# RWKV-7 chain of a hybrid block: stacked 128-row operands, loads in two parts, token operands by head half

## The chip, the cores and the metric

The kernel runs on one core of a Trainium2 chip. Its time is the device time of one execution in microseconds (us); lower is better. The kernel before takes 5299.23 us (median of 3 runs).

## What is computed

A block: one layer over 2048 latent tokens and 256 context tokens: a token mixer with two groups of heads side by side (HGRN2 and RWKV-7, each in both directions), an output projection, and a mixture of experts. The change touches the RWKV-7 part alone: 8 heads of 64, each with a 64x64 state, walked forward and backward.

```python
def rwkv7_scan(r, w, k, v, kk, a, s0):
    def step(s, inp):
        rt, wt, kt, vt, kkt, at = inp
        sa = jnp.einsum('nbhij,nbhj->nbhi', s, kkt)
        s = (s * wt[..., None, :] - sa[..., :, None] * (kkt * at)[..., None, :]
             + vt[..., :, None] * kt[..., None, :])
        return s, jnp.einsum('nbhij,nbhj->nbhi', s, rt)
...
def rwkv7_readout(y, r, k, v, g, r_k, gn_w, gn_b):
...
    yn = ((y - mu) * lax.rsqrt(var + RW_GN_EPS)).reshape(y.shape[:-2] + (D_RW,)) * gn_w + gn_b
    bonus = jnp.sum(r * k * r_k, -1, keepdims=True) * v
    return (yn + bonus.reshape(bonus.shape[:-2] + (D_RW,))) * g
```

## The kernel before

Everything is float32; one matmul shows as two records in the profile. The stages follow one another: modulation, RWKV projection, HGRN projection beside RWKV preparation (`RwkvPrep`), the two scans side by side (`scans`, about 1,540 to 3,240 us of the span), readout (`Readout`), experts, combination.

**Preparation** writes two scratch tensors to DRAM. `s_rw_in` holds, per direction and chunk of 64 tokens, rows of 1028 numbers with the channel (two heads of 64, a "pair") on 128 partitions: alpha, rho, decay, beta, kappa. `s_rw_tm` holds the token-major operands (64 tokens by beta, kappa, v, 512 channels each).

**The RWKV scan** (`RwkvScan`) takes 36 steps of 64 tokens, each for two directions d = 0 and 1. Heads lie in 4 pairs j; half h = 0 or 1 of a pair is on partitions 0 to 63 or 64 to 127. The body for step n does two things: it builds the operands and the triangular inverse of step n (`gram0`, `gram1`, `turn`, then `cross` and `grow` for levels 1 to 5), and runs the state chain of step n-1 on the other set of buffers (`rhs`, `solve`, `out`, `state`):

- `rhs`: alpha times state plus masked kappas times v (L1370, L1372), copied by ScalarE (ACT);
- `solve`: inverse times rhs gives u (L1381), copied by ScalarE (L1488);
- `out`: rho times state, plus kappas times v, plus A_rho_beta times u (L1391, L1393, L1395);
- `state`: kappa tokens times v plus beta tokens times u (L1405, L1407); VectorE (DVE) adds the state (L1583) and multiplies by the decay (L1585).

`mask(d, 1)` on VectorE (L1560, to `rw_kappas`) masks what `gram1` (L1422) left in PSUM, in one instruction; `turn` (L1431) waits for it. GpSimd (POOL) makes the level masks of the inverse (L1544), VectorE its first level (L1569) and its later ones (L1575).

**The HGRN scan** is interleaved on all engines: 18 steps, one per two RWKV steps, from a quarter of the first of the two bodies on. Its scores (L429) need operands scaled by GpSimd (L411, L412), from exponents by VectorE (L474) and ScalarE (L379, L380).

**Order.** The order on each engine is a list of positions (`RW_ORDER`, below) merged with the HGRN tasks when the program is built; every engine runs its own list in order and waits on semaphores. A loop iteration holds four RWKV and two HGRN steps. Below, an *even body* is one with u = 0, an *odd body* one with u = 1; the HGRN output phase ends just ahead of an even body.

```python
RW_ORDER = ("gram0 rhs gram1 turn cross1 solve grow1 cross2 out grow2 cross3 grow3 state cross4 grow4 cross5 grow5").split()
```

**Loads.** SyncE (SP) issues the loads of step n once `s_ready` says that VectorE has finished the state of body n-1: per direction one DMA of `rw_operands` (128 rows of 4112 bytes) and two of `rw_tokens` (pieces of 256 bytes), all counted on one semaphore, for which `gram0` waits.

## Time and profile before

| | |
|---|---|
| median of 3 runs | 5299.23 us (5294.71 to 5325.04) |
| the profiled execution, its own time | 5331.71 us |
| its span in the trace | 5329.8 us |
| granted TensorE clock, mean over the span | 0.913 of full speed |
| TensorE (PE) busy | 4381.7 us, 82% |
| VectorE busy | 2250.0 us, 42% |
| ScalarE busy | 1214.9 us, 23% |
| GpSimd busy | 1510.6 us, 28% |

Busy time is the union of an engine's instructions. Records of matmuls overlap, so the time that a matmul adds is read from the distance of the starts of consecutive groups, not from the duration of one.

### The profile page before, as it was taken

The numbers are of one execution on the slowest core, as the hardware profiler recorded it, in microseconds if no ns is written. First come the engines' busy times: TensorE is split into PE (matmuls) and PEld (weight loads), VectorE is DVE, ScalarE is ACT, GpSimd is POOL, SyncE is SP. The second block draws the span as 40 slices with busy tenths as digits, with TensorE's granted clock in tenths as the row PEclk, the third lists the DMA queues.
The fourth block names the chain that finished last, engine by engine and source line by source line (L and its number), as shares of the span: only waits on it lengthen the run. The fifth ranks groups of instructions, "written<-read, shape, count | busy, mean of one in ns | idle before, by whom it ended". The sixth has DMA issues, their size and how long they took to land. (4 is left out here: it accounts for less than half of the span.)

```text
span 5329.8 us, 123036 instructions
## 1 busy us (share of the span) xinstructions
PE 4381.7 (82%) x47298; PEld 2984.8 (56%) x47298; DVE 2250.0 (42%) x4072; ACT 1214.9 (23%) x3101; POOL 1510.6 (28%) x1933
## 2 busy tenths in 40 slices
PE   3998799899969888988888885875699999999950
PEld 1877666666658777877777773443233333333320
DVE  1112176666644544544445444887111111111138
ACT  0001044443433333333333332321000000000000
POOL 0000011011125544545445453443222212222210
PEclk7999899999989999999999997987899999999975
DMA  9312255555533232232322325432757798887864
GB/s 302 126 58 71 67 184 194 163 179 187 167 94 90 70 82 62 70 90 70 88 60 68 89 70 149 141 132 82 291 228 283 323 370 365 363 364 325 340 242 185
DMA packets 365510, 917.20 MB, mean 172 GB/s; under 512 B 181121, under 2 KB 220417, under 8 KB 332065
## 3 DMA queue, kind: packets, MB, share of 16 engines
q1 hardware_dynamic: 310208, 760.24, 41.2%
q0 software_dynamic: 47392, 133.02, 7.1%
q10 hardware_dynamic: 7488, 17.83, 0.9%
q8 instruction: 326, 5.34, 0.4%
q14 instruction: 96, 0.78, 0.0%
HBM read 951.35 MB, written 211.26 MB: 218 GB/s over the span
## 5 line engine op out<-in xcount | busy, mean ns | idle before, releaser
L2405 PE MATMUL exp_gate_up<-exp_w_gate,exp_rows_and_rowsT 128*64 128x512 f32 x1664 | 773.2, 624 | 89.9 <-DMA exp_w_up<-in_moe_w_up_dram 89.0
L2405 PE MATMUL exp_gate_up<-exp_w_up,exp_rows_and_rowsT 128*64 128x512 f32 x1664 | 773.9, 624 | 0.0
L2405 PEld LDWEIGHTS exp_gate_up<-exp_w_gate,exp_rows_and_rowsT 128*64 128x64 f32 x1664 | 235.9, 144 | 592.7 <-issue 592.7
L1544 POOL TENSOR_TENSOR rw_A_level<-rw_A_rho_beta,const_level_masks 128x256 f32<-128x256 f32 x432 | 336.7, 795 | 705.4 <-DVE rw_A_rho_beta L1560 428.8
L721 PE MATMUL rwp_product<-rwp_hT,rwp_w_rw 128*128 128x256 f32 (+1 forms) x2016 | 443.9, 383 | 0.0
L874 PE MATMUL hgp_product<-hgp_hT,const_w_hg 128*128 128x256 f32 x1728 | 410.4, 394 | 26.6 <-DMA hgp_hT<-s_hT 15.8
L2359 DVE TENSOR_TENSOR exp_hidden<-exp_hidden,exp_gate_up 64x512 f32<-64x512 f32 x104 | 71.9, 692 | 821.9 <-ACT exp_hidden L2340 821.9
L721 PEld LDWEIGHTS rwp_product<-rwp_hT,rwp_w_rw 128*128 128x128 f32 (+1 forms) x2016 | 380.9, 189 | 61.2
L874 PEld LDWEIGHTS hgp_product<-hgp_hT,const_w_hg 128*128 128x128 f32 x1728 | 337.6, 199 | 87.8 <-DMA hgp_hT<-s_hT 16.3
L2429 PE MATMUL exp_down<-exp_w_down,exp_hiddenT 128*64 128x512 f32 x1664 | 380.0, 598 | 1.1
L1575 DVE TENSOR_TENSOR rw_inverse<-rw_inverse,rw_inverse_bank 128x512 f32<-128x512 f32 x288 | 196.5, 685 | 356.8 <-PE rw_inverse_bank L1454 354.8
L2340 ACT ACTIVATE exp_hidden<-exp_gate_up 64x512 f32<-64x512 f32 x104 | 61.2, 588 | 1075.1 <-PE exp_gate_up L2405 1075.1
L2313 POOL DMA_INDIRECT s_yb<-exp_out,exp_row_slot x104 | 104.2, 1002 | 677.2 <-PE exp_rows_turned L2391 552.2
L1451 PE MATMUL rw_inverse_bank<-rw_inverse,rw_X 64*64 64x64 f32 x5760 | 246.2, 227 | 60.3 <-ACT rw_X L1504 40.2
L1443 PE MATMUL rw_inverse_bank<-rw_inverse,rw_A_level 64*64 64x64 f32 x5760 | 231.9, 222 | 45.8 <-DVE rw_inverse L1575 37.3
L1451 PEld LDWEIGHTS rw_inverse_bank<-rw_inverse,rw_X 64*64 64x64 f32 x5760 | 211.1, 140 | 74.2 <-issue 68.0
L411 POOL TENSOR_TENSOR hg_scaled_qk<-hg_qkf,hg_exponent 128x256 f32<-128x256 f32 x252 | 217.3, 862 | 121.7 <-ACT hg_exponent L380 121.4
L871 PE MATMUL hgp_product<-const_w_hg,hgp_hT 128*128 128x512 f32 x576 | 251.6, 592 | 0.0
L2009 PE MATMUL read_projected<-read_w_out,read_mixT 128*128 128x512 f32 x512 | 235.9, 621 | 4.1 <-DVE read_w_out L1874 2.9
L1504 ACT ACTIVATE rw_X<-rw_inverse_bank 128x256 f32<-128x256 f32 x360 | 135.2, 380 | 452.9 <-PE rw_inverse_bank L1443 447.3
L1443 PEld LDWEIGHTS rw_inverse_bank<-rw_inverse,rw_A_level 64*64 64x64 f32 x5760 | 199.0, 135 | 67.2 <-issue 58.9
L2405 PEld LDWEIGHTS exp_gate_up<-exp_w_up,exp_rows_and_rowsT 128*64 128x64 f32 x1664 | 235.8, 144 | 0.0
(385 smaller groups left out, 7942.8 us busy)
## 6 DMA issues: line engine op xcount, KB each, us to landing
exp_w_gate<-in_moe_w_gate_dram SPq DMA_DIRECT2D x104, 2048.0 KB
exp_w_up<-in_moe_w_up_dram SPq DMA_DIRECT2D x104, 2048.0 KB
exp_w_down<-in_moe_w_down_dram SPq DMA_DIRECT2D x104, 2048.0 KB
s_rw_in<-prep_operands SPq DMA_DIRECT2D x72, 514.0 KB, 4.1
rw_operands<-s_rw_in SPq DMA_DIRECT2D x72, 514.0 KB, 5.5
rw_tokens<-s_rw_tm SPq DMA_DIRECT2D x144, 192.0 KB, 6.6
hg_qkf<-s_hg_in SPq DMA_DIRECT2D x36, 768.0 KB, 7.9
mod_w<-in_w_mod_dram SPq DMA_DIRECT2D x24, 1024.0 KB, 26.1
```

The costliest lines, as they stand in the source:

```text
L411: nc.gpsimd.tensor_tensor(zk, level_views(k, d, l)[1], dk, ALU.mult)
L721: mm = nc.tensor.matmul(mp[o % 2][0:width, 0:GROUP], w_in[:, k, c0 - 5 * D_HG:c0 - 5 * D_HG + width], hT[b][:, k, :], start=(k == 0), stop ...
L871: mm = nc.tensor.matmul(self.mp[o % 4][:], self.hT[b][:, k, j * P:(j + 1) * P], self.w[:, k, c0:c0 + D_HG], start=(k == 0), stop=(k == KD ...
L874: mm = nc.tensor.matmul(self.mp[o % 4][:, 0:GROUP], self.w[:, k, c0:c0 + P], self.hT[b][:, k, :], start=(k == 0), stop=(k == KD - 1))
L1443: i = nc.tensor.matmul(self.pa[d][q, 0, j, :], self.al[d][l % 2][q, j, :], self.rt[u][d][q, 1, j, :], start=True, stop=True)
L1451: i = nc.tensor.matmul(self.pa[d][q, 0, j, :], self.x[d][q, j, :], self.rt[u][d][q, 0, j, :], start=True, stop=True)
L1504: nc.scalar.activation(self.x[d][:], self.pa[d][:, 0], ACT.Copy).then_inc(s["x_ready"], 1)
L1544: nc.gpsimd.tensor_tensor(self.al[d][l % 2][:], self.ar[u][d][:, :, 0, :], self.K["lvc"][:, d, l, :].unsqueeze(1).broadcast_to([P, NPAIR, ...
L1575: V.tensor_tensor(rt[:], rt[:], self.pa[d][:], ALU.add).then_inc(s["r_ready"], 1)
L2009: mm = self.nc.tensor.matmul(self.py[j][:], self.mT[:, k, :], self.w_out[:, k, j * 512:(j + 1) * 512], start=(k == 0), stop=(k == KD - 1))
L2405: i = nc.tensor.matmul(pgu[u][q:q + BLK], xT[:, k, r * BLK:(r + 1) * BLK], w[r][:, k, :], start=(k == 0), stop=(k == KD - 1))
L2429: i = nc.tensor.matmul(pd[u][c * 64 + x:c * 64 + x + BLK], hT[u][:, k, x:x + BLK], wd[r][:, k, c * 512:(c + 1) * 512], start=(k == 0), sto ...
```

## The change

Instead of two or three matmuls with 64 rows that add up in PSUM, one matmul with 128 rows takes both terms, with the operands stacked on the partitions. Per step and direction:

- `lead` holds, for half h of each pair, alpha and rho on that half's partitions and the masked kappas on the other half's; `sv` holds state over v, `uv` u over v, `tk` beta tokens over kappa tokens. `rhs` falls from 16 matmuls to 8, `out` from 24 to 16 (8 with 128 rows, then 8 with 64 for the u term, pair by pair), `state` from 16 to 8. `gram1` writes to the other half's partitions.
- The mask of the kappas becomes two VectorE instructions of 64 partitions, the state's add and decay two each, ScalarE's copy of u two.
- A step's loads are 22 DMAs in place of 6. Alpha and rho are issued after `y_ready`, the rest of the row after `s_ready`, then for both directions the tokens with a semaphore of their own, for which only the next body's `rhs` waits. v is loaded twice.
- `s_rw_tm` is laid out by operand and head half (pieces of 1 KB). ScalarE's copies in the preparation write in that order; the readout loads v in it and adds the bias into a new tile `v_bias`.

```diff
-        self.row = two(lambda u, d: sb(f"operands{u}{d}", [P, ROW]))
-        self.tm = two(lambda u, d: sb(f"tokens{u}{d}", [P, 3, NPAIR, RW_C]))
+        self.lead = two(lambda u, d: sb(f"alpha_rho_over_kappas{u}{d}", [P, 2, 2, NPAIR, RW_C]))
+        self.row = two(lambda u, d: sb(f"decay_beta_kappa{u}{d}", [P, ROW - 2 * XW]))
+        self.tk = two(lambda u, d: sb(f"beta_over_kappa_tokens{u}{d}", [P, 2, NPAIR, RW_C]))
+        self.sv = two(lambda u, d: sb(f"state_over_v{u}{d}", [P, 2, NPAIR, RW_C]))
+        self.uv = two(lambda u, d: sb(f"u_over_v{u}{d}", [P, 2, NPAIR, RW_C]))
...
     def sync(self, sp, n, u):
...
+            wait(sp, s["y_ready"], n - 1)
+            row = S["rw_in"][d, bass.ds(n, 1)].rearrange("n p x -> p (n x)")
+            for h in range(2):
+                sp.dma_start(self.lead[u][d][HALF[h], h].rearrange("p x j t -> p (x j t)"), row[HALF[h], 0:2 * XW]).then_inc(got, 16)
             wait(sp, s["s_ready"], n - 1)
...
+            sp.dma_start(self.row[u][d][:], row[:, 2 * XW:]).then_inc(got, 16)
+        for d in range(2):
+            tok = S["rw_tm"][d, bass.ds(n, 1)].rearrange("n x h s e -> x h s (n e)")
             for h in range(2):
...
+                for x in range(2):
+                    sp.dma_start(self.tk[u][d][HALF[h ^ x], h].rearrange("s j e -> s (j e)"), tok[x, h]).then_inc(self.tokens[u][d], 16)
+                for v in (self.sv, self.uv):
+                    sp.dma_start(v[u][d][HALF[1 - h], h].rearrange("s j e -> s (j e)"), tok[2, h]).then_inc(self.tokens[u][d], 16)
...
         def rhs(d):
...
+            pe.wait_ge(self.tokens[w][d], self.got_tokens(n - 1, w))
             pe.sem_inc(self.turns, 1)
...
+            for j, h, q in places:
+                i = nc.tensor.matmul(self.pb[d][q, 0, j, :], self.lead[w][d][:, h, 0, j, :], self.sv[w][d][:, h, j, :], start=True, stop=True)
...
         def out(d):
...
+                for _, h, q in places[0:2]:
+                    nc.tensor.matmul(o[q, 0, j, :], self.lead[w][d][:, h, 1, j, :], self.sv[w][d][:, h, j, :], start=True, stop=False)
+                for _, h, q in places[0:2]:
+                    i = nc.tensor.matmul(o[q, 0, j, :], self.ar[w][d][q, j, 1, :], self.uv[w][d][q, h, j, :], start=False, stop=True)
...
         def mask(d, k):
...
+            for h in range(2):
+                q = HALF[1 - h]
+                i = V.tensor_tensor(self.lead[u][d][q, h].rearrange("p x j t -> p j x t"), grams[q],
+                                    K["bu"][q, d].unsqueeze(1).broadcast_to([RW_C, NPAIR, 2, RW_C]), ALU.mult)
+            i.then_inc(s["masked"], 1)
...
         def state(d):
...
+            for h in range(2):
+                q = HALF[h]
+                V.tensor_tensor(self.st[d][q], self.sv[w][d][q, h], self.pb[d][q, 1], ALU.add).then_inc(s["s_order"], 1)
+            dve.wait_ge(s["s_order"], 2 * n)
+            for h in range(2):
+                q = HALF[h]
+                i = V.tensor_tensor(self.sv[u][d][q, h], self.st[d][q], self.row[w][d][q, 0:NPAIR].unsqueeze(2).broadcast_to([RW_C, NPAIR, RW_C]),
+                                    ALU.mult)
```

TensorE at the start of `out(0)` in an even body. Before: the last two cross products (direction 0 and 1), then one pair's three terms of two matmuls each, which repeat for the other pairs and direction 1.

```order
L1443 MATMUL rw_inverse_bank0<-rw_inverse00,rw_A_level00 64x64 x8
L1443 MATMUL rw_inverse_bank1<-rw_inverse01,rw_A_level10 64x64 x8
L1391 MATMUL rw_chain_bank0<-rw_state0,rw_operands10 64x64 x2
L1393 MATMUL rw_chain_bank0<-rw_tokens10,rw_kappas10 64x64 x2
L1395 MATMUL rw_chain_bank0<-rw_u0,rw_A_rho_beta10 64x64 x2
```

After: the same two cross products, then one 128-row term and one 64-row term per pair, in turn.

```order
L1455 REGISTER_ALU
L1458 MATMUL rw_inverse_bank0<-rw_inverse00,rw_A_level00 64x64 x8
L1458 MATMUL rw_inverse_bank1<-rw_inverse01,rw_A_level10 64x64 x8
L1413 MATMUL rw_chain_bank0<-rw_state_over_v10,rw_alpha_rho_over_kappas10 64x64 x2
L1415 MATMUL rw_chain_bank0<-rw_u_over_v10,rw_A_rho_beta10 64x64 x2
```

The three terms of a pair became two, and kinds with 128 and 64 rows alternate eight times per direction.

SyncE between the state of one body and the next HGRN loads (L353). Before, one step's loads for both directions:

```order
L1343 DMA rw_operands<-s_rw_in 128x1028
L1345 DMA rw_tokens<-s_rw_tm 64x12x64 x2
L1343 DMA rw_operands<-s_rw_in 128x1028
L1345 DMA rw_tokens<-s_rw_tm 64x12x64 x2
L353 DMA hg_qkf<-s_hg_in 128x3x512
```

After, the same stretch:

```order
L1356 DMA rw_alpha_rho_over_kappas<-s_rw_in 64x512 x2
L1358 DMA rw_decay_beta_kappa<-s_rw_in 128x516
L1356 DMA rw_alpha_rho_over_kappas<-s_rw_in 64x512 x2
L1358 DMA rw_decay_beta_kappa<-s_rw_in 128x516
L1363 DMA rw_beta_over_kappa_tokens<-s_rw_tm 64x256 x2
L1365 DMA rw_state_over_v<-s_rw_tm 64x256
L1365 DMA rw_u_over_v<-s_rw_tm 64x256
```

The three kinds of token rows at the end stand four times in a row, once per direction and half; then come the HGRN loads, L353. So the tokens stand behind both directions' rows now.

VectorE at the start of an even body, from the mask of `gram0` to the first later level of the inverse. Before:

```order
L1560 TENSOR_TENSOR rw_A_rho_beta<-rw_inverse_bank,const_before_upto 128x512 x2
L1569 TENSOR_TENSOR rw_inverse<-rw_A_level,const_ident 128x256 x2
L1560 TENSOR_TENSOR rw_kappas<-rw_inverse_bank,const_before_upto 128x512 x2
L1575 TENSOR_TENSOR rw_inverse<-rw_inverse,rw_inverse_bank 128x512 x2
L497 SCALAR_TENSOR_TENSOR hg_logf_sum<-const_chunk_starts,hg_logf 128x512 x2
```

After:

```order
L1578 TENSOR_TENSOR rw_A_rho_beta<-rw_inverse_bank,const_before_upto 128x512 x2
L1593 TENSOR_TENSOR rw_inverse<-rw_A_level,const_ident 128x256 x2
L1583 TENSOR_TENSOR rw_alpha_rho_over_kappas<-rw_inverse_bank,const_before_upto 64x4x2x64 x4
L1599 TENSOR_TENSOR rw_inverse<-rw_inverse,rw_inverse_bank 128x512 x2
L497 SCALAR_TENSOR_TENSOR hg_logf_sum<-const_chunk_starts,hg_logf 128x512 x2
```

The mask of the kappas has four instructions for its two, ahead of the same work.

## Rows read from the trace of the kernel before

**Rows 1.** The page, part 1: busy time and share of the span.

```profile
PE 4381.7 (82%) x47298; PEld 2984.8 (56%) x47298; DVE 2250.0 (42%) x4072; ACT 1214.9 (23%) x3101; POOL 1510.6 (28%) x1933
```

**Rows 2.** Windows, the scan without its ends: busy time by engine, clock, DMA share.

```profile
1560.00:3220.00 1660.00, 1457.52 (x34204) 1295.12 (x34203) 814.04 (x1438) 573.27 (x1500) 863.94 (x1070) 0.95 0.28 73
```

**Rows 3.** Waits in the same stretch: us in total, times, longest.

```profile
PE rw_inverse_bank L1451 <- ACT rw_X L1504: 40.2, 18, 2.4
...
PE rw_inverse_bank L1422 <- DMA rw_tokens<-s_rw_tm: 35.2, 19, 2.8
...
PE rw_inverse_bank L1431 <- DVE rw_kappas L1560: 10.6, 15, 1.4
```

**Rows 4.** Timeline, TensorE, 16-record groups: start, length, line, tile shape, count.

```profile
2352.07 0.63 PE L1451 MATMUL rw_inverse_bank<-rw_inverse,rw_X 64*64 64x64 f32 x16
2352.53 0.63 PE L1454 MATMUL rw_inverse_bank<-rw_X,rw_inverse 64*64 64x64 f32 x16
2353.10 0.69 PE L429 MATMUL hg_score_psum<-hg_scaled_qk 128*64 128x64 f32 x16
2353.71 0.68 PE L1451 MATMUL rw_inverse_bank<-rw_inverse,rw_X 64*64 64x64 f32 x16
2354.23 0.63 PE L1454 MATMUL rw_inverse_bank<-rw_X,rw_inverse 64*64 64x64 f32 x16
```

**Rows 5.** Timeline, TensorE in the HGRN output phase, where the tile shape changes.

```profile
2371.28 0.43 PE L452 MATMUL hg_out_psum<-hg_v,hg_scores_across 128*64 128x128 f32 x2
2371.64 0.43 PE L454 MATMUL hg_out_psum<-hg_v,hg_scores 64*64 64x128 f32 x4
```

**Rows 6.** Timeline, TensorE, two terms of `out`.

```profile
2394.52 0.31 PE L1391 MATMUL rw_chain_bank<-rw_state,rw_operands 64*64 64x64 f32 x4
2394.64 0.31 PE L1393 MATMUL rw_chain_bank<-rw_tokens,rw_kappas 64*64 64x64 f32 x4
```

**Rows 7.** Timeline, the start of an even body, by engine.

```profile
2385.33 1.80 DVE L1569 TENSOR_TENSOR rw_inverse<-rw_A_level,const_ident 128x256 f32<-128x256 f32 x2 [0.33 <-POOL rw_A_level L1544]
...
2385.67 1.92 PE L1422 MATMUL rw_inverse_bank<-rw_operands 64*64 64x128 f32 x32
...
2387.05 1.28 DVE L1560 TENSOR_TENSOR rw_kappas<-rw_inverse_bank,const_before_upto 128x512 f32<-128x512 f32 x2
...
2387.88 1.24 PE L1431 MATMUL rw_inverse_bank<-const_ident,rw_inverse 64*64 64x64 f32 x32 [0.29 <-DVE rw_kappas L1560]
```

**Rows 8.** Timeline, the start of an odd body, by engine.

```profile
2421.49 1.09 PE L1422 MATMUL rw_inverse_bank<-rw_operands 64*64 64x128 f32 x16 [2.15 <-DMA rw_tokens<-s_rw_tm]
2421.87 0.84 POOL L412 TENSOR_TENSOR hg_scaled_qk<-hg_qkf,hg_exponent 128x256 f32<-128x256 f32 x1
...
2423.44 0.69 PE L429 MATMUL hg_score_psum<-hg_scaled_qk 128*64 128x64 f32 x16
...
2427.02 0.69 DVE L1560 TENSOR_TENSOR rw_kappas<-rw_inverse_bank,const_before_upto 128x512 f32<-128x512 f32 x1 [1.37 <-PE rw_inverse_bank L1422]
...
2427.89 0.69 DVE L1560 TENSOR_TENSOR rw_kappas<-rw_inverse_bank,const_before_upto 128x512 f32<-128x512 f32 x1 [0.18 <-PE rw_inverse_bank L1422]
...
2428.40 1.15 PE L1431 MATMUL rw_inverse_bank<-const_ident,rw_inverse 64*64 64x64 f32 x32
```

**Rows 9.** Timeline, VectorE around the state of an even body.

```profile
2410.07 0.43 DVE L1585 TENSOR_TENSOR rw_state<-rw_state,rw_operands 128x256 f32<-128x256 f32 x1
...
2412.32 0.69 DVE L1575 TENSOR_TENSOR rw_inverse<-rw_inverse,rw_inverse_bank 128x512 f32<-128x512 f32 x1 [0.90 <-PE rw_inverse_bank L1454]
```

**Rows 10.** DMA issues in the scan: KB each, median us from issue to landing.

```profile
rw_operands<-s_rw_in SPq DMA_DIRECT2D x68, 514.0 KB, 5.1
rw_tokens<-s_rw_tm SPq DMA_DIRECT2D x136, 192.0 KB, 6.5
```

**Rows 11.** Windows, ten microseconds around an odd body's load wait.

```profile
2326.00:2336.00 10.00, 7.56 (x126) 6.69 (x123) 5.13 (x10) 1.78 (x6) 5.06 (x8) 0.83 0.41 94
```

**Rows 12.** Timeline, the first matmuls of the scan.

```profile
1543.38 1.97 PE L1422 MATMUL rw_inverse_bank<-rw_operands 64*64 64x128 f32 x16 [35.35 <-DMA rw_tokens<-s_rw_tm]
```

91 lines of the change are left out of this document (41 added, 50 removed).

## Prediction

> **What bounds the kernel now.** I read the page first: TensorE is busy 82% of the span, no other engine over 42% [rows 1]. The change lies in the scan, so the next view is the window of 1560 to 3220 us: TensorE 1457.5 of 1660 us busy, VectorE 814, GpSimd 864, ScalarE 573, DMA share 0.28, clock 0.95 [rows 2]. TensorE leads, but it isn't alone. It runs one list in order, and its gaps name three others: ScalarE's `rw_X` 40.2 us, a load 35.2 us, the mask of the kappas 10.6 us [rows 3]. So each edit has two prices, in TensorE's stream and in the wait that ends last near it, and I read one even body and one odd body as timelines for the second.
>
> **TensorE's stream.** In `out` the next term starts 0.117 us after four records, that is two 64-row matmuls: 0.058 us for a matmul [rows 6]. A group of 16 records (8 matmuls) takes 0.46 to 0.47 us start to start in one tile shape [rows 4]. The 128-row price is in the HGRN scores: L429 has 128x64 tiles, 64 columns wide, in alternate halves, just as the new matmuls. Around it the distances are 0.46, 0.57, 0.61 and 0.52 us [rows 4]. Against 0.467 that is 0.30 too much for two changes of tile shape, so a stacked matmul costs the same 0.058 us, and a change of shape 0.15 us. The HGRN output confirms this: four 64-row records of 128 columns, or two of 128 rows, take 0.36 us there [rows 5], where `gram` pays about 0.056 us a record (32 records in about 1.8 us) and so 0.225 for four; the rest, 0.14, is the change of shape.
>
> I counted both programs' lists over one loop iteration (four steps): 1936 matmuls become 1744, and changes of shape rise from 113 to 179. 192 x 0.058 = 11.2 us are saved, 66 x 0.15 = 9.9 us are added. Net -1.3 us per four steps, -12 us over the scan's nine iterations. By place, per body: `out` saves 8 x 2 x 0.058 = 0.93 us and adds 16 changes (15 in an odd body, where L429 stands ahead), +1.3 to +1.5 us. `rhs` and `state` each save 0.93 us less 0.30 us for the changes, or the whole 0.93 where L429 stands beside them.
>
> The page "TensorEngine Tiling (Array Packing)" of the Trainium skill, section "Restrictions and Gotchas", says that row tiles can't access the same PSUM bank at once. By it the pairs of 64-row tiles would take turns and the stacked ones not, so that the 192 stacked matmuls per iteration would take half: 192 x 0.029 x 9, a further 50 us off. Rows 4 speak against it: L1451 (64 rows) and L429 (128 rows) go at one pace. Its section "Tiling Modes" says that a change of tile within a mode needs no drain, which is what the `gram1` that writes across does; no run here shows such a tile. The nearest rows bound that edit between 0 and 0.15 us a change, and I take 0, since the shape is the same.
>
> **The mask split in two.** `turn` waits for it. In the even body VectorE is in L1569 until 2387.13, starts the masks at 2387.05 and ends them 1.28 us later; `turn` starts at 2387.88, 0.14 us behind the first one's end [rows 7]. Two masks are 1.28 us with 0.69 each [rows 8], so one more costs 0.60. The half-height ones have the same length per partition; I take the full 0.60 us each (0.30 would be in proportion to partitions, no row shows it). Two more make the second `turn` 1.2 us later. The time that a shorter `rhs` gives is lost here too: `gram1` ends earlier, but VectorE, not TensorE, is late (L1569 waited for GpSimd [rows 7]). Even body up to `turn`: +1.2 us.
>
> **The load wait.** In odd bodies the second `gram0` waits for the tokens, 2.15 us in the row, 1.85 us on the mean of 19 [rows 3, 8]. After the change it waits only for the row, issued ahead of the tokens; a row lands 5.1 us after issue, tokens 6.5 [rows 10]. The state of the even body ends at 2410.5 [rows 9], so the rows land by about 2417.5, ahead of 2419.3, where the wait began. The wait goes. Next late is the HGRN: L429 at 2423.44 needs L412, which ends at 2422.71 [rows 8], and that doesn't move. So only 0.6 of the 2.15 us come through, and the shorter first `rhs` brings nothing more. Then the second `rhs` saves 0.35 us, `gram1` begins near 2424.9, the masks run from 2425.95 to 2428.45, and the second `turn` starts at 2428.55, where it started at about 2428.95 (half of the 1.15 us behind 2428.40). Odd body up to `turn`: -0.4 us. Where the clock fell around the wait (0.83 granted over ten microseconds [rows 11], the lower level for a third of them) more comes back, for all was twice as long; I saw this in about 8 of 18, at 1.5 us, -12 us in all.
>
> **State.** TensorE's 0.93 us saved stands ahead of HGRN scores that wait themselves, so I keep half. VectorE has eight instructions for four; the second of a pair adds about 0.35 us, 1.3 us a body. Behind them are HGRN exponents and the inverse of level 4, which had 0.90 us of slack [rows 9]: +0.3 us. The page "SBUF — State Buffer" of the Trainium skill says that a VectorE operation with two SBUF inputs and a GpSimd one lock each other out; the multiplication has two such inputs. The row agrees in kind (L1569 took 0.90 us a piece beside GpSimd, [rows 7]). By it the split would cost up to 1 us more a body.
>
> **Edits taken at nothing.** ScalarE's second copy of u (0.4 us a piece) lies 3 us ahead of `out`, under `grow1` and `cross2`. 22 DMAs for 6 on SyncE: their tokens are needed a body later, and the HGRN loads behind them half a body later; if a DMA costs 0.5 us to issue that is 11 us of 47 a body. In preparation and readout the same elements move in another order, beside a busy TensorE. At the scan's start the first `gram0` comes with the row in place of the tokens, 1.4 us sooner [rows 10, 12], and the second doesn't wait (some 1.85 us): -3 us.
>
> **The sum.** Even body: +1.2 (turn) +1.5 (out) -0.5 (state, half) +0.3 (VectorE) = +2.5 us. Odd body: -0.4 +1.3 -0.5 +0.3 = +0.7 us. 18 of each: +58 us; less 12 (clock) and 3 (start): +43 us. Some of what I add will fall into waits that were there (`rw_X` 40.2 us, [rows 3]), though its ScalarE work starts behind `out` and so moves along; I take off a quarter, 11 us. Forecast **+32 us**: the profiled execution's 5331.7 would be 5364, the median 5299 would be 5331.
>
> **Rivals.**
> - *TensorE's stream decides and the waits vanish.* -12 us of stream, -35 of load wait, -12 of clock, -3 at the start, masks hidden: -62, 5237 us. For it: TensorE is the busiest. Against it: in both timelines another engine ends last at `turn` and L429. Chance 0.12.
> - *Split instructions land on the chain in full* (slower). Each body pays the masks (1.2 us even; 0.7 odd, where they start 0.87 us apart and `turn` had some 0.2 us), VectorE's state (1.3) and `out` (1.5, 1.3), and keeps nothing of `rhs` and `state`: 18 x (4.0 + 3.3) = +131; less 15 (clock, start) and 11 (0.6 us of the load wait in 18 bodies) and the same quarter: +79, 5378 us. It decides from the point where VectorE's extra 2.5 us a body exceeds its slack. Chance 0.22.
> - *The changes of shape cost little in short groups*, say half: -66 x 0.075 x 9 = -45 from the forecast, 5286 us. The price is from groups of 2 to 16 records, so it is well held. Chance 0.14.
> - *PSUM rule* (the page above): 5281 us. Chance 0.02.
> - The forecast, near 5331: chance 0.50.
>
> **How the numbers follow.** Under 1% (53 us) this kernel's runs can't tell from no change. The forecast's own spread (a state saving kept or lost, VectorE at 0.3 to 1.3 us) is +-30 us. The range runs from 5255, which leaves out most of the first rival, to 5395, which takes in most of the second. Faster by over 1% (under 5246): 0.13. Slower by over 1% (over 5352): a quarter of the forecast's own chance and most of the second rival's, 0.34. Within: 0.53.
>
> **What would show it.** Right: the load wait of `gram0` gone; waits on the kappa mask up from 10.6 us to 40 or more; groups in `out` 0.26 us apart; new waits ahead of L429 in odd bodies. Wrong: masks of half height near 0.3 us; groups in `out` 0.12 to 0.2 us apart; the scan shorter by tens of microseconds with the waits on VectorE unchanged; or a clock that falls more often, since `out` now leaves gaps in the array.

## The result and the profile after

The changed kernel takes 5378.72 us (median of 4 runs, 5366.24 to 5383.47), the kernel before 5297.33 us (4 runs). By the medians that is 81 us more; the ratio is 1.0143, 95% interval 1.0119 to 1.0168, that is 76 us (63 to 89), where 32 was forecast. The sign was right, the forecast less than half of what came; the time fell on the slower rival (5378).

The page, part 1, of the kernel after, and windows over the whole scan, before and after:

```profile
PE 4364.3 (81%) x43842; PEld 2940.6 (55%) x43842; DVE 2392.4 (44%) x4290; ACT 1247.9 (23%) x3173; POOL 1528.3 (28%) x1933
...
1543.38:3232.28 1688.90, 1481.12 (x34551) 1314.68 (x34553) 820.97 (x1454) 577.15 (x1509) 869.87 (x1078) 0.95 0.29 75
1540.12:3291.22 1751.10, 1468.49 (x31152) 1267.85 (x31152) 961.98 (x1666) 609.50 (x1580) 886.40 (x1078) 0.94 0.26 78
```

From the first `gram0` to the end of the last `solve` the scan takes 1751.1 us where it took 1688.9: +62. In it TensorE is busy only 13 us less, for all the matmuls saved, and VectorE 141 us more; the granted clock is 0.94 for 0.95. This scan length is the measure for the experiments below. It comes from one profiled execution of each kernel, and that of the kernel before (5331.71) lies 34 us over its median, where the others lie at most 11 us from theirs; so set beside its 1688.9 another kernel looks somewhat faster than it is. The start comes 3.3 us sooner, as forecast (3), and what stands behind the scan is 9.5 us shorter in these two profiles, which the change doesn't touch beyond the readout.

The waits of TensorE from 1560 to 3220 us, as in [rows 3], of the kernel after (us in total, times, longest; the last 71 us of the scan lie behind this stretch):

```profile
PE rw_inverse_bank L1458 <- DVE rw_inverse L1599: 85.7, 94, 2.8
PE rw_inverse_bank L1466 <- ACT rw_X L1521: 42.5, 18, 2.4
PE rw_inverse_bank L1446 <- DVE rw_alpha_rho_over_kappas L1583: 41.5, 31, 1.8
PE rw_inverse_bank L1437 <- issue: 30.3, 7, 5.3
PE rw_inverse_bank L1446 <- issue: 27.8, 37, 1.4
```

The load wait of [rows 3], 35.2 us, is gone, and the wait for `rw_X` is what it was (40.2). Three others have come or grown: `turn` (L1446) waits for the kappas' mask (10.6 before) and, in the row "issue", for its second half; the `cross` products (L1458) wait for the inverse (L1599); and `gram0` (L1437) stands still seven times for nothing that these rows name, once per loop iteration (10.7 us in seven times before).

The start of an even body, the place of [rows 7], in the timeline after:

```profile
2416.18 1.80 DVE L1593 TENSOR_TENSOR rw_inverse<-rw_A_level,const_ident 128x256 f32<-128x256 f32 x2 [0.34 <-POOL rw_A_level L1561]
2418.01 2.81 DVE L1583 TENSOR_TENSOR rw_alpha_rho_over_kappas<-rw_inverse_bank,const_before_upto 64x512 f32<-64x512 f32 x4
2419.55 0.68 PE L1446 MATMUL rw_inverse_bank<-const_ident,rw_inverse 64*64 64x64 f32 x16 [1.75 <-DVE rw_alpha_rho_over_kappas L1583]
2420.93 0.68 PE L1446 MATMUL rw_inverse_bank<-const_ident,rw_inverse 64*64 64x64 f32 x16 [0.70 <-issue]
```

Four half masks take 2.81 us where two whole ones took 1.28: (2.81 - 0.69) / 3 = 0.71 us apart, not 0.60. The second `turn` starts 2.92 us behind the first mask. Before, its 32 records had no gap.

`out` (0.26 us a term, as forecast), from the timeline after, and below it the state section of an odd body:

```profile
2427.14 0.34 PE L1413 MATMUL rw_chain_bank<-rw_state_over_v,rw_alpha_rho_over_kappas 128*64 128x64 f32 x4
2427.41 0.33 PE L1415 MATMUL rw_chain_bank<-rw_u_over_v,rw_A_rho_beta 64*64 64x64 f32 x4
...
2441.12 1.10 PE L1423 MATMUL rw_chain_bank<-rw_u_over_v,w_beta_over_kappa_tokens 128*64 128x64 f32 x32
2442.16 0.68 PE L1458 MATMUL rw_inverse_bank<-rw_inverse,rw_A_level 64*64 64x64 f32 x16
...
2442.43 0.86 DVE L1609 TENSOR_TENSOR rw_state_sum<-rw_state_over_v,rw_chain_bank 64x256 f32<-64x256 f32 x2
2443.32 0.85 DVE L1613 TENSOR_TENSOR rw_state_over_v<-rw_state_sum,rw_decay_beta_kappa 64x256 f32<-64x256 f32 x2
2444.20 0.87 DVE L1609 TENSOR_TENSOR rw_state_sum<-rw_state_over_v,rw_chain_bank 64x256 f32<-64x256 f32 x2
2445.10 1.28 DVE L1613 TENSOR_TENSOR rw_state_over_v<-rw_state_sum,rw_decay_beta_kappa 64x256 f32<-64x256 f32 x2
2446.42 0.69 DVE L474 TENSOR_TENSOR hg_exponent<-hg_logf_sum 128x512 f32<-128x512 f32 x1
...
2447.48 1.27 DVE L1599 TENSOR_TENSOR rw_inverse<-rw_inverse,rw_inverse_bank 128x512 f32<-128x512 f32 x2
2448.40 1.19 PE L1458 MATMUL rw_inverse_bank<-rw_inverse,rw_A_level 64*64 64x64 f32 x32 [1.85 <-DVE rw_inverse L1599]
```

TensorE's state product is now 1.04 us from start to start, a saving; but VectorE needs from 2442.43 to 2446.38 for the eight halves, each as long as the whole instruction of [rows 9]. Then come an HGRN exponent and the inverse. In [rows 9], of an even body, VectorE waited 0.90 us at this point for TensorE; now TensorE waits 1.85 us for VectorE.

The start of an odd body, the place of [rows 8]:

```profile
2451.96 1.96 PE L1437 MATMUL rw_inverse_bank<-rw_alpha_rho_over_kappas,rw_decay_beta_kappa 64*64 64x128 f32 x32
2454.93 0.69 PE L429 MATMUL hg_score_psum<-hg_scaled_qk 128*64 128x64 f32 x16
2455.60 1.03 POOL L412 TENSOR_TENSOR hg_scaled_qk<-hg_qkf,hg_exponent 128x256 f32<-128x256 f32 x1
```

Both `gram0` run without a gap. L429 starts while the L412 that I took for its releaser has not begun.

Worked out from the traces: the median, over 17 even bodies (without the first) and 18 odd ones, of the time from direction 0's first matmul of a position to direction 0's first of the next position, where the row doesn't say otherwise. The row `rhs` ends at `gram1`, and an HGRN score can lie in between.

| from, to | even before | even after | odd before | odd after |
|---|---|---|---|---|
| `gram0`(0) to `gram0`(1) | 0.92 | 0.92 | 3.25 | 0.92 |
| `rhs`, both directions | 1.86 | 1.08 | 3.56 | 2.29 |
| `gram1` to `turn` | 2.20 | 3.70 | 2.46 | 4.15 |
| `turn`(0) to `turn`(1) | 0.55 | 1.38 | 0.52 | 1.38 |
| `out` | 2.80 | 4.12 | 2.85 | 4.07 |
| `state` | 2.09 | 1.03 | 2.58 | 1.55 |
| `grow4` to `cross5` | 2.58 | 4.61 | 2.67 | 4.14 |

### The profile page after: what moved, and what is told of

Same layout as the page of the kernel before. It is cut to its first block and busy times, and to the rows that moved or that the text cites. A ratio compares the mean times of both kernels' runs of the same rounds, so it can differ in the third digit from the quotient of the medians.

```text
span 5379.2 us, 117918 instructions
## 1 busy us (share of the span) xinstructions
PE 4364.3 (81%) x43842; PEld 2940.6 (55%) x43842; DVE 2392.4 (44%) x4290; ACT 1247.9 (23%) x3173; POOL 1528.3 (28%) x1933
## 5 line engine op out<-in xcount | busy, mean ns | idle before, releaser
L1599 DVE TENSOR_TENSOR rw_inverse<-rw_inverse,rw_inverse_bank 128x512 f32<-128x512 f32 x288 | 195.6, 684 | 363.2 <-PE rw_inverse_bank L1469 361.8
L1458 PE MATMUL rw_inverse_bank<-rw_inverse,rw_A_level 64*64 64x64 f32 x5760 | 250.8, 230 | 96.0 <-DVE rw_inverse L1599 90.7
L1466 PE MATMUL rw_inverse_bank<-rw_inverse,rw_X 64*64 64x64 f32 x5760 | 253.2, 232 | 55.1 <-ACT rw_X L1521 42.5
L1458 PEld LDWEIGHTS rw_inverse_bank<-rw_inverse,rw_A_level 64*64 64x64 f32 x5760 | 214.7, 142 | 119.7 <-issue 112.1
```

Of the source, the lines that this page charges most:

```text
L1458: i = nc.tensor.matmul(self.pa[d][q, 0, j, :], self.al[d][l % 2][q, j, :], self.rt[u][d][q, 1, j, :], start=True, stop=True)
L1466: i = nc.tensor.matmul(self.pa[d][q, 0, j, :], self.x[d][q, j, :], self.rt[u][d][q, 0, j, :], start=True, stop=True)
L1599: V.tensor_tensor(rt[:], rt[:], self.pa[d][:], ALU.add).then_inc(s["r_ready"], 1)
```

## Experiments

Ratios are to the runs of the kernel before on the same chip, with 95% intervals, and its median differs by up to 18 us from one set to the next, so kernels are compared by ratios where the two disagree; "scan" is the scan length of the profiled run.

| | kernel | us | ratio | scan |
|---|---|---|---|---|
| | before | 5297.33 | 1 | 1688.9 |
| | changed | 5378.72 | 1.0143 [1.0119, 1.0168] | 1751.1 |
| e1 | before, kappas' mask in halves | 5367.46 | 1.0109 [1.0085, 1.0133] | 1727.2 |
| e9 | before, kappas' mask twice, whole | 5342.65 | 1.0058 [1.0032, 1.0084] | 1710.2 |
| e2 | before, state add and decay in halves | 5304.57 | 0.9984 [0.9968, 1.0000] | 1666.5 |
| e3 | before, loads in two parts | 5278.52 | 0.9935 [0.9911, 0.9959] | 1645.9 |
| e5 | e3 and e2 | 5277.41 | 0.9931 [0.9910, 0.9952] | 1648.8 |
| e14 | e3, tokens in 16 DMAs | 5252.38 | 0.9890 [0.9852, 0.9927] | 1612.9 |
| e6 | e3, `state` stacked | 5231.10 | 0.9842 [0.9808, 0.9875] | 1604.3 |
| e10 | e6 and e2 | 5298.40 | 0.9980 [0.9966, 0.9995] | 1664.6 |
| e4 | changed, `out` with half the shape changes | 5349.00 | 1.0069 [1.0042, 1.0095] | 1722.4 |
| e11 | changed, masks in another order | 5367.38 | one run | 1731.7 |
| e7 | changed, mask whole | 5284.88 | 0.9948 [0.9929, 0.9967] | 1702.8 |
| e8 | e7, state add and decay whole | 5228.35 | 0.9837 [0.9802, 0.9872] | 1620.8 |
| e12 | changed, HGRN loads first | 5394.67 | 1.0149 [1.0109, 1.0188] | 1763.6 |
| e13 | e6, HGRN loads first | 5275.44 | 0.9930 [0.9899, 0.9961] | 1645.9 |

**e1, the mask alone.** In the kernel before:

```diff
+            for h in range(2):
+                q = HALF[1 - h]
+                i = V.tensor_tensor(dst[q], grams[q], K["bu"][q, d].unsqueeze(1).broadcast_to([RW_C, NPAIR, 2, RW_C]), ALU.mult)
+            i.then_inc(s["masked"], 1)
```

> The kernel before with one edit: VectorE masks the kappas of gram1 in two instructions of 64 partitions for one of 128; everything else stays. Theory A (the split instructions of VectorE make the change slower): the changed kernel's trace has two such halves 0.71 us apart, four in a row 2.84 us where two whole ones took 1.29. The second turn comes 1.5 us later in even bodies and about 1.1 us later in odd ones: 18 x 2.6 = +48 us, 5345 us; waits of TensorE on the mask rise from 10.6 us to 40 or more. Rival B (the loss is in TensorE's changes of tile shape, the masks are mostly covered): +0 to +15 us. Rival C (as the prediction put it, 0.60 us a half): +1.2 and +0.7, 18 x 1.9 = +34 us.

The one small edit costs 1.09%, 58 us, three quarters of what the whole change costs. An even body in the timeline of e1:

```profile
2404.44 2.81 DVE L1566 TENSOR_TENSOR rw_kappas<-rw_inverse_bank,const_before_upto 64x512 f32<-64x512 f32 x4
...
2405.98 0.68 PE L1431 MATMUL rw_inverse_bank<-const_ident,rw_inverse 64*64 64x64 f32 x16 [1.10 <-DVE rw_kappas L1566]
2407.36 0.68 PE L1431 MATMUL rw_inverse_bank<-const_ident,rw_inverse 64*64 64x64 f32 x16 [0.69 <-issue]
```

It is the picture of the kernel after, without any of its other edits: 2.81 us of masks, two `turn` groups 1.38 us apart.

**e9, the same number of instructions at full height.**

```diff
+            for dst in (self.kk_spare[d], self.kk[u][d]):
+                i = V.tensor_tensor(dst[:], grams, K["bu"][:, d].unsqueeze(1).broadcast_to([P, NPAIR, 2, RW_C]), ALU.mult)
+            i.then_inc(s["masked"], 1)
```

> The kernel before with the kappas mask done twice, each time by one instruction over all 128 partitions, the first time into a spare tile. As many more VectorE instructions as in e1 (one per direction and step), at full height. Theory A (an extra instruction costs its length wherever its height is, and half-height ones are held a little longer: 0.71 us apart against 0.60): starts of the masks about 0.60 us apart, second kappas mask of direction 1 1.8 us behind the first one of direction 0; VectorE ends its four 0.3 us sooner than in e1, so 18 x 2 x 0.6 to 1.0: +35 to +50 us over before, scan about 1720 us against 1727 in e1. Theory B (half height itself is what is dear, and a whole instruction more is mostly hidden): under +15 us. Theory C (dearer than e1, for its two instructions read and write twice as much): +65 or more.

```profile
2392.24 0.68 DVE L1566 TENSOR_TENSOR rw_kappas_spare<-rw_inverse_bank,const_before_upto 128x512 f32<-128x512 f32 x1
2392.84 0.68 DVE L1566 TENSOR_TENSOR rw_kappas<-rw_inverse_bank,const_before_upto 128x512 f32<-128x512 f32 x1
```

The four starts are 0.60 us apart (two shown), and the kernel loses 31 us (0.58%, interval 17 to 45). Twice the elements, and yet cheaper than the halves of e1 by 27 us: the height saves nothing, and the halves stand further apart (0.71). Theory A held for the starts; its +35 to +50 us was a little high. The times bear the 0.60 us an instruction that I had forecast, and the rest of e1 comes with the halves: in the traces the second `turn` comes 0.46 us (even) and 0.33 us (odd) later than in e9, 18 x 0.79 = 14 us, the scan is 17 us longer, and the 27 us of the times carry some 13 us of noise each.

**e11, the order of the halves.**

```diff
-            for h in range(2):
+            for h in ((0, 1), (1, 0))[d]:
```

> The changed kernel with direction 1's two mask halves in reverse order, so that the second and third of the four instructions work on the same 64 partitions. If the 0.71 us between starts comes from switching partitions, the middle distance falls to about 0.60 us; if it comes from half height or from the form of the operands, all three stay at 0.71. Time as the changed kernel, 5379 within 15 us.

```profile
2410.70 2.69 DVE L1583 TENSOR_TENSOR rw_alpha_rho_over_kappas<-rw_inverse_bank,const_before_upto 64x512 f32<-64x512 f32 x4
```

Now the middle two of the four work on the same partitions, and the group is 0.12 us shorter (2.69 for 2.81): in all groups the middle distance is 0.61 us, and the outer two are 0.71 and 0.69. So the 0.11 us extra is paid where an instruction changes the half of the partitions, not for the half height. The time (one run) is within what was expected of no change.

**e3, the loads.** The tokens are issued behind both rows, on a semaphore of their own, with the old tiles and layout:

```diff
-    N_LOADS = 3
+    N_LOADS, N_TOKENS = 1, 2
...
-                sp.dma_start(self.tm[u][d][h * RW_C:(h + 1) * RW_C], tok[h]).then_inc(got, 16)
+                sp.dma_start(self.tm[u][d][h * RW_C:(h + 1) * RW_C], tok[h]).then_inc(self.tokens[u][d], 16)
...
+            pe.wait_ge(self.tokens[w][d], self.got_tokens(n - 1, w))
```

> The kernel before with the load part alone: the tokens have a semaphore of their own, for which the next body's rhs waits, and are issued behind both directions' rows; layouts, sizes and the 6 DMAs stay. Theory A: the load wait of odd bodies comes through in full, as it seems to in the changed kernel's trace: 18 x 2.1 + 3 at the start = -41 us, 5256 us. Rival (the prediction: the HGRN scores wait for GpSimd's L412, so only 0.6 us of each comes through, and some clock): 18 x 0.6 + 12 + 3 = -26 us, 5271 us or nearer to the kernel before.

It gains 34 us (interval 22 to 47). The load wait leaves the list, and the wait that I had expected to take its place grows by less:

```profile
PE rw_inverse_bank L1448 <- DVE rw_inverse L1580: 39.1, 90, 0.8
PE hg_score_psum L429 <- issue: 34.1, 36, 2.5
```

L429's gaps were 21 us in the kernel before, so 13 of the 35 us went there; the rest is gained, with some low clock.

**e2 and e5, the state's halves.** VectorE's add and decay in two instructions of 64 partitions each, in the kernel before (e2) and in e3 (e5):

```diff
+            for h in range(2):
+                q = HALF[h]
+                V.tensor_tensor(self.st[d][q], self.st[d][q], self.pb[d][q, 1], ALU.add).then_inc(s["s_order"], 1)
+            dve.wait_ge(s["s_order"], 2 * n)
```

> The kernel before with one edit: VectorE's add and multiply of the state are two instructions of 64 partitions each. Theory A (split instructions): 4 more instructions a body at 0.44 us start to start in the changed kernel's trace, 1.76 us a body, less 0.9 us of slack ahead of the inverse of level 4: +0.9 x 36 = +31 us, 5328 us, and cross5 (L1443) waits longer for VectorE (L1575). The prediction's term (+0.3 a body): +11 us. Rival B (loss in the changes of shape): 0.

> The kernel before with two edits: loads in two parts (as in e3) and VectorE's state operations in halves (as in e2). Alone, the halves moved nothing (0.998), while the load wait of odd bodies fell from 35 to 19 us and the wait of cross5 on VectorE rose from 37 to 74. Theory D (the later state was paid out of the load wait that stood behind it): without that wait it costs 1.6 us in even and 0.4 us in odd bodies, 18 x 2.0 = +36 us over e3, 5314 us, no faster than the kernel before. Rival: the halves have slack of their own and cost nothing here too, 5278 us as e3.

Neither costs anything: 0.9984, and 0.9931 against e3's 0.9935. The halves are seen, since the wait for the inverse doubles (e5, 39.1 in e3), and L429's gaps give it back (34.1 in e3):

```profile
PE rw_inverse_bank L1448 <- DVE rw_inverse L1580: 75.0, 115, 1.9
PE hg_score_psum L429 <- issue: 15.2, 15, 1.6
```

The halves' delay itself is there (in even bodies `grow4` to `cross5` takes 4.22 us for e3's 2.58); it is paid back at other places, and what L429's gaps are stands under e12 to e14. At this point VectorE's state looked innocent.

**e6, the state product alone stacked.** e3, with beta tokens over kappa tokens and u over v, `rw_tm` by head half with its preparation and readout, ScalarE's copy of u in halves; `rhs`, `out`, the mask and VectorE's state as before:

```diff
-                    nc.tensor.matmul(o[q, 1, j, :], tm[q, 1, j, :], tm[q, 2, j, :], start=True, stop=False)
-                for _, q in heads[0:2]:
-                    i = nc.tensor.matmul(o[q, 1, j, :], tm[q, 0, j, :], self.uu[d][q, j, :], start=False, stop=True)
+                    i = nc.tensor.matmul(self.pb[d][q, 1, j, :], self.tk[w][d][:, h, j, :], self.uv[w][d][:, h, j, :], start=True, stop=True)
```

> The kernel before with loads in two parts and the stacked form for the state product alone: beta over kappa tokens times u over v, 8 matmuls of 128 rows for 16 of 64, tokens by head half in DRAM, ScalarE's u copy in halves. rhs and out keep their 64-row terms, and no VectorE instruction is split. Theory D (stacking pays where it needs no split VectorE instruction): state saves 0.93 us a body beside an HGRN score of the same tile shape, 36 x 0.93 = -33 us against e3, 5245 us. Rival (the saving falls into waits of the HGRN scores behind it, as the prediction took for half): -10 to -17 us, 5262 to 5268 us.

5231 us: 1.6% faster than the kernel before, 2.7% faster than the changed one (3.0% by the ratios), and the best of this study. Against e3 it gives another 0.9%, 49 us. I put all of that down to the stacked product, until e14 (below) showed that half of it is the tokens' 16 DMAs. What is left for the product, 0.48%, is within the intervals of the two ratios, and by the scans it is 9 us (1612.9 to 1604.3).

**e10, e6 with the state's halves.** The edit of e2 in e6.

> e6 (before with loads in two parts and the state product alone stacked, 5231 us) with the state's add and decay on VectorE in two 64-partition instructions each, as the changed kernel has them. Theory A (a shorter state product on TensorE makes VectorE the late one at the last level of the inverse, so that here the halves cost what they did not cost behind the longer product of e5): +35 to +57 us over e6, so 5266 to 5288, the waits of the last cross on VectorE's inverse near 75 us or more, its load wait still gone. Theory B (halves are as free here as in e5 against e3): 5231, within 10 us. Theory A also says that the stacking of the state product then saves next to nothing against e5 (5277).

It loses 67 us by the medians (1.4% by both), more than theory A's 57, and is even slower than e5, which does without the stacking. The same place in e6 and in e10, the state section of an odd body; first e6:

```profile
2359.61 0.40 DVE L1602 TENSOR_TENSOR rw_state<-rw_state,rw_chain_bank 128x256 f32<-128x256 f32 x1
...
2360.83 0.42 DVE L1604 TENSOR_TENSOR rw_state<-rw_state,rw_operands 128x256 f32<-128x256 f32 x1
...
2362.83 0.69 DVE L1594 TENSOR_TENSOR rw_inverse<-rw_inverse,rw_inverse_bank 128x512 f32<-128x512 f32 x1 [0.64 <-PE rw_inverse_bank L1471]
```

and e10:

```profile
2300.15 0.86 DVE L1604 TENSOR_TENSOR rw_state<-rw_state,rw_chain_bank 64x256 f32<-64x256 f32 x2
...
2302.83 1.36 DVE L1608 TENSOR_TENSOR rw_state<-rw_state,rw_operands 64x256 f32<-64x256 f32 x2
...
2305.28 1.28 DVE L1594 TENSOR_TENSOR rw_inverse<-rw_inverse,rw_inverse_bank 128x512 f32<-128x512 f32 x2
...
2306.20 1.01 PE L1460 MATMUL rw_inverse_bank<-rw_inverse,rw_A_level 64*64 64x64 f32 x26 [1.80 <-DVE rw_inverse L1594]
```

In e6 VectorE is through with the state in 1.64 us and still waits 0.64 us for TensorE; in e10 it needs 4.04 us and TensorE waits 1.80. The median from `grow4` to `cross5` goes from 2.76 to 4.46 us in even bodies and from 2.68 to 4.14 in odd ones; after the change it is 4.61 and 4.14. The total of that wait, e6 and e10 in turn:

```profile
PE rw_inverse_bank L1460 <- DVE rw_inverse L1594: 46.0, 83, 1.9
```

```profile
PE rw_inverse_bank L1460 <- DVE rw_inverse L1594: 102.7, 104, 3.0
```

57 us more, for 60 of scan. Part of that is the clock. Windows over the scan of e6 and of e10:

```profile
1537.35:3141.68 1604.33, 1415.46 (x33424) 1261.93 (x33424) 842.00 (x1454) 606.91 (x1580) 885.38 (x1078) 0.97 0.27 85
```

```profile
1538.07:3202.67 1664.60, 1435.66 (x33424) 1280.72 (x33424) 909.34 (x1594) 606.39 (x1580) 881.60 (x1078) 0.95 0.27 82
```

The matmuls are the same, 33424 records, the granted clock is 0.97 and 0.95, and TensorE is busy 20 us longer in e10: about that much is the clock.

The pair e3 and e5 has the same edit without the stacked product, and its scan grows by 3 us only. Set beside it, e10 shows how much the meeting of the two edits explains. In even bodies `grow4` to `cross5` grows by as much in both pairs (1.64 and 1.70 us); in odd ones by 0.43 us without the stacking and by 1.46 with it. The two losses of scan differ by 57 us (60 and 3). Of these the wait for the inverse gives 21 (it grows by 57 us here and by 36 there), and TensorE's busy time 32 (20 us more here, 12 less there). This part goes with the clock (0.95 to 0.96 there), and no run shows why the clock moves.

**e4, shape changes in `out`.** The changed kernel, with the order of the two terms turned in every second pair, so that terms of one shape meet: 10 changes of shape for 16, 9 for 15.

```diff
+                one, other = (stacked, single) if j % 2 == 0 else (single, stacked)
+                one(j, True)
+                i = other(j, False)
```

> The changed kernel with out in another order: for pairs 1 and 3 the 64-row term comes first, so that equal tile shapes meet. 10 changes of shape per body for 16 (9 for 15 in odd bodies). Theory (0.15 us a change, all on the path): -0.9 x 36 = -32 us against the changed kernel's 5379, so 5347 us. Rival (changes of shape are cheap in short groups, or the time falls into a wait behind out): 0 to -10 us.

```profile
2363.87 0.45 PE L1413 MATMUL rw_chain_bank<-rw_u_over_v,rw_A_rho_beta 64*64 64x64 f32 x8
2364.25 0.45 PE L1411 MATMUL rw_chain_bank<-rw_state_over_v,rw_alpha_rho_over_kappas 128*64 128x64 f32 x8
```

Four matmuls of one shape and one change: 0.38 us, which is 4 x 0.058 + 0.15. `out` falls from 4.12 and 4.07 us to 3.20 and 3.14, 0.92 us for six changes (0.15 each), and the kernel by 30 us (medians, 39 by the ratios; the scan is 29 shorter, and 18 x 1.85 = 33). So `out` is on the path in full, within the noise, and the price of a change is what I read.

**e7 and e8, VectorE's work whole again.** The changed kernel with one mask of 128 partitions into a tile of its own (e7), and with the state's add and decay whole too (e8):

```diff
+            V.tensor_tensor(self.kk[u][d][:], grams, K["bu"][:, d].unsqueeze(1).broadcast_to([P, NPAIR, 2, RW_C]),
+                            ALU.mult).then_inc(s["masked"], 1)
```

> The changed kernel with the kappas of gram1 masked by one VectorE instruction of 128 partitions, into a tile of its own; the kappas in the stacked operand stay zero, so the terms of the kappas times v are left out of the result. Same matmuls, same loads, same order. Theory A (the two halves cost what they cost alone, +57 us in e1): 5379 - 57 = 5322 us. Rival (in the changed kernel the earlier rhs uncovers more: gram1 ends sooner, turn then waits for nothing): up to 2.0 us a body, 5307 us.

> As e7, and VectorE's add and multiply of the state are one instruction of 128 partitions each too, in a tile of their own; the state in the stacked operand stays zero, so the state terms are left out of the result as well. What stays of the change is stacked matmuls, loads in two parts and the u copy in halves. Theory D: a further 36 us off e7, 5271 to 5286 us; by its parts from the kernel before (5310 in the last set): loads -34, out +47, rhs and state -30 each gives 5263 us. Rival (the state halves cost nothing, as alone in e2): the same as e7.

Leaving terms out sends tokens to other experts, and that stage gets shorter; so only the scan counts here, and whether operands that stay zero move the clock is not shown. Whole masks take 48 us off it (1751.1 to 1702.8), whole state instructions a further 82 (to 1620.8), and the wait of `cross` for the inverse goes from 98.4 us (e7) to 30.7 (e8). Without VectorE's six extra instructions a body, the rest of the change makes the scan 68 us shorter than before.

**e12, e13 and e14, the loads' place.** The summed parts left 29 us open, and I had taken the 22 DMAs at nothing. After the change SyncE needs until 1912 us for the sixteen token DMAs of an even step, and the HGRN loads come behind them; the kernel after, SyncE and then TensorE:

```profile
1912.56 0.39 SPq L353 DMA_DIRECT2D hg_qkf<-s_hg_in  x1
...
1915.42 0.35 SPq L354 DMA_DIRECT2D hg_v<-s_hg_v  x1
...
1923.34 1.97 PE L1437 MATMUL rw_inverse_bank<-rw_alpha_rho_over_kappas,rw_decay_beta_kappa 64*64 64x128 f32 x16 [5.32 <-issue]
```

In the trace's records of TensorE's queue, the branch that closes the loop takes 7.1 us here (from 1915.8) and 5.0 to 7.1 us in all seven, where it takes 3.4 to 3.8 before, with the HGRN loads issued some 20 us ahead of it (1889.3 to 1894.7, branch at 1910.5). Of the kernels so far it is slow in all that load the tokens in 16 DMAs and in no other. e12 and e13 set the HGRN loads ahead of the even step's RWKV loads, in the changed kernel and in e6; e14 is e3 with the same tokens in 16 DMAs:

```diff
-                        r.sync(sp, 2 * k, 0)
                         h.sync(sp, k, u)
+                        r.sync(sp, 2 * k, 0)
```

> The changed kernel with SyncE's list in another order: the HGRN loads of an iteration's half stand ahead of the even step's RWKV loads, not behind its sixteen token DMAs. In the changed kernel the branch that closes TensorE's loop takes 5.0 to 7.1 us, seven times in the scan, where it takes 3.3 to 3.8 us before; while it runs, the DMA engines are busy with the 2 MB of HGRN loads, which the token DMAs have pushed back to that point (issued 1912.6 to 1915.8, the branch from 1915.8; before they were issued 1889.3 to 1894.7 and the branch came at 1911). Theory L (that traffic holds up the fetch of TensorE's code): the branches fall to near 3.4 to 4.5 us, the gaps ahead of the even bodies' gram0 by 1.5 to 3 us seven times, and some of the low clock behind them goes: 10 to 25 us faster than 5379. Theory M (the branch is longer because the program is laid out otherwise): the branches stay at 5 to 7 us, time as the changed kernel within 6 us.

> e6 (loads in two parts, the state product alone stacked, 5231 us; loop branches of 5.7 to 6.1 us) with the HGRN loads ahead of the even step's RWKV loads. Theory L (HGRN traffic holds up the fetch at the loop's end): branches near 3.4 to 4.5 us and 5206 to 5221 us. Theory M (the layout of the program): branches as in e6, 5231 within 6 us.

> e3 (before with loads in two parts, 5279 us, loop branches of 3.3 to 3.9 us) with the same token bytes in 16 DMAs a step instead of 4, by pair; nothing else is changed, TensorE's program is the same as e3's. Theory L: the HGRN loads are issued 6 us or more later, near the loop's end, and the branches grow to 5 us or more, 10 to 25 us slower than e3. Theory M (branches are longer by the layout of TensorE's program): branches stay at 3.3 to 3.9, and the time as e3 within 6 us, so that 12 more DMAs a step are free.

Of the branch theory L is right: it falls to 3.4 to 3.8 us in e12, 3.3 to 3.8 in e13, and grows to 5.9 to 6.4 in e14, whose program for TensorE is that of e3. Of the time it is wrong in all three: e12 is no faster than the changed kernel, e13 is 44 us slower than e6, and e14 is 26 us faster than e3. In e13, TensorE stops in the middle of a body instead, from 2307.4 to 2311.4, 3 us behind the HGRN loads:

```profile
2302.44 0.39 SPq L353 DMA_DIRECT2D hg_qkf<-s_hg_in  x1
...
2311.41 0.86 PE L429 MATMUL hg_score_psum<-hg_scaled_qk 128*64 128x64 f32 x11 [3.81 <-issue]
```

```profile
2307.40:2311.40 4.00, 0.20 (x5) 0.12 (x4) 1.43 (x2) 0.81 (x3) 2.68 (x4) 1.00 0.67 250
```

The windows' row, of these 4 us, has TensorE at 0.20 us and the DMA engines at 0.67. The gap lies between two weight loads of one product with no semaphore between. The trace's queue named "instruction" brings a block of 16 KB every 5.2 us (median). Here one starts at 2299.3 and the next at 2309.1, 9.8 us later, and TensorE goes on 2.3 us behind that. So the traffic holds TensorE's code up wherever it falls; at the loop's end it falls on a wait that is there in any case. In odd bodies of e13 `grow1` to `cross2` takes 7.27 us for 3.78 (medians), 18 times, which is the whole loss and more. "Runtime: NRT & Kernel Launch" of the Trainium skill, section "Instruction fetch mechanics", calls the crossing of a block mostly hidden and a taken branch a stall; the branch's 3.4 us agrees, and with the DMA engines this busy the crossing is not hidden: 3.8 us.

The same test says what the other gaps named "issue" are, in the kernel before too. Its scan has 59 of more than 0.3 us; 58 of them end 2.1 to 3.4 us behind the start of such a block, a distance at which only 23% of its matmuls start. So I read them as waits for code. With what `gram0` waits behind the branch they come to 64 us in the kernel before, and to the following in others:

| | before | e3 | e5 | e14 | e6 | e10 | e13 | e12 | changed |
|---|---|---|---|---|---|---|---|---|---|
| waits for code, us | 64 | 70 | 47 | 66 | 83 | 65 | 104 | 60 | 63 |
| of it at `gram0` behind the branch | 11 | 11 | 13 | 30 | 29 | 27 | 10 | 13 | 30 |
| TensorE at the lower clock, us of the scan | 177 | 153 | 119 | 92 | 102 | 153 | 144 | 222 | 194 |

L429's gaps are part of the first row. Where TensorE has to stand for VectorE, it stands less for its code: e5 waits 36 us more than e3 for the inverse and 24 less for code, e10 57 more than e6 and 18 less. In e12 the wait only moves, from `gram0` (30 to 13 us) into the bodies (33 to 47).

Why e14 beats e3 I can only say by where it shows. Its waits for code are about as long in all (66 us for 70), since what the gaps ahead of L429 lose (34.1 in e3) `gram0` gains. What is left is the clock of its scan, 0.97 (0.95 in e3), with TensorE busy 26 us less, of 33 us of scan:

```profile
PE hg_score_psum L429 <- issue: 14.8, 20, 1.4
```

## Why the prediction was wrong

The mechanism of most terms was right, and the one that decides, the state's, was mis-sized. The chain of scan lengths shows it: from the kernel before to e6 (loads, tokens, `state` stacked) -84.6 us, to e8 (`rhs` and `out` stacked, the rest of the loads) +16.5, to e7 (the state's halves) +82.0, to the changed kernel (the masks' halves) +48.3, together +62. By the table above, with 18 bodies of each kind and beside the forecast's own terms: up to the second `turn` +9 us where +14 was forecast, `out` +46 for +50, and the state +25 for -7. The state's miss of 32 us is the largest. These 80 us, with 20 more that `gram0` waits for code, are more than the 62: 21 come back in shorter waits for code in the bodies, and 17 I can't place in these medians.

In ratios, each step measured beside its neighbour: loads -0.65% (e3), tokens in 16 DMAs -0.45% (e14), `state` stacked -0.48% (e6 against e14), the state's halves on it +1.38% (e10 against e6), the masks +1.09% (e1), together +0.89%; the changed kernel stands at +1.43%. The 0.54% left, 29 us, is for `out` and `rhs`, which I didn't try alone: by the table `out` adds 18 x (1.32 + 1.22) = 46 us and `rhs` saves up to 18 x (0.78 + 1.27) = 37, which leaves 9; e6 to e8 has 17. The differences carry some 0.3% each.

- **`out`, +1.5 and +1.3:** right; 1.32 and 1.22 us, and e4 bears the 0.15 us.
- **The mask, +1.2 even and -0.4 odd with the load wait:** the term was too small. An instruction costs its 0.60 us, as forecast (e9: +31 us for 36 bodies x 1.2 less what lies in waits), but the halves start 0.71 us apart. In the even body the second `turn` starts 2.92 us behind the first mask, and 1.38 before (it follows 2387.88 by 0.55 [rows 7]): 1.54 for the 1.2. In the odd body I let the masks vanish in slack: `gram1` to the second `turn` grew there by 1.69 + 0.86 = 2.55 us. In all, 58 us alone (e1); my masks were at most 36 x 1.2 = 43 and mostly netted against other savings. The net came near all the same, by luck: up to the second `turn` the even body is 1.55 us longer and the odd one 1.05 us shorter, since the load wait (next) gave back what the masks took.
- **The load wait, 0.6 of 2.15 us:** wrong, to the other side. All of it came through (3.25 to 0.92 in the table, 34 us in e3). "L429 at 2423.44 needs L412, which ends at 2422.71" was an inference from their nearness: [rows 8] show no wait at that L429, and after the change it starts before that L412. What stood behind the load wait in part was code (L429's gaps, 21 us before and 34 in e3). Of the signs named ahead, the vanished load wait, over 40 us for the mask (41.5) and the 0.26 us in `out` came; new waits ahead of L429 didn't, its gaps fell from 21 to 3 us.
- **State, half of 0.93 kept and +0.3 for VectorE:** the step that failed. It was to save 0.2 us a body, 7 us in all. TensorE saves 1.06 and 1.03 us, more than I kept, but `grow4` to `cross5` grows by 2.03 and 1.47, so that the state section costs 0.97 us in even bodies and 0.44 in odd ones, 25 us in all. VectorE's halves alone cost 60 us of scan in e10 and 82 from e8 to e7, where +0.3 a body is 11. The slack of 0.90 us [rows 9] was measured with TensorE's product long. The stacking takes 1.0 us off TensorE's side of the race and the halves add 2.4 us (e10, 4.04 for 1.64) on VectorE's; the two edits meet at one point, and each alone is free or a gain (e5, e6). The meeting is what the traces show in odd bodies, and about a third of what the halves cost with the stacking and not without; in even bodies the halves come 1.64 us late even in e5, where shorter waits for code and a better clock paid for them. I had taken 0.35 us for the second of a pair, where 0.43 to 0.44 was paid, and 1.3 us a body, of which 0.3 late. The page "SBUF — State Buffer" of the Trainium skill, section "Who interferes with whom", bears on one part: it has a VectorE instruction with two SBUF inputs contend with a GpSimd one that reads SBUF. The trace agrees: two decays take 1.28 us at 2445.10, where GpSimd's L412 runs beside them, for 0.85 at 2443.32.
- **22 DMAs at nothing:** wrong, but to neither side in sum. They push the HGRN loads to the loop's end, where `gram0` waits 30.3 us for TensorE's code (10.7 before); yet the same displacement gains 0.45% in e14.
- **Clock, -12:** it didn't come. The clock of the scan is 0.95 before and 0.94 after, the lower level holds for 177 us and for 194.
- **The quarter in old waits, -11:** right in kind, at another place than `rw_X` (40.2 and 42.5 us). The waits for code away from `gram0` fell from 53 to 33 us, and those at `gram0` took 20 back.
- **The rivals.** "Split instructions land on the chain in full" gave the number and was nearer in kind, but hit it by luck: it kept nothing of `rhs` and `state` and 11 us of the load wait, where the load wait gave all and both the halves' costs were larger. "TensorE's stream decides" (-62) is near what the change is without VectorE's splits (e8, -68 of scan). The rule on one PSUM bank at once, from the page "TensorEngine Tiling (Array Packing)" of the Trainium skill, section "Restrictions and Gotchas", is not borne out as a cost here: 16 stacked matmuls of `state` take 1.04 us start to start (0.065 each, with a shape change in it), the pace of the 64-row pairs in [rows 6], 0.058.

What stays open: where the rest of the 29 us lies, of which the scans give `rhs` and `out` 17; what the stacked `state` product is worth by itself; and why the scan's clock is better when the HGRN loads come at the loop's end and worse with the halves on the stacked product.
